# First head group of a chunked scan on TensorE: two heads in one product, unread full-height products between

## The chip, the cores and the metric

One core of a Trainium2 chip. The metric is the device time of one execution in microseconds (us), the median of three runs. The trace is one further execution, taken by the hardware profiler; all instants below are us from its start. TensorE runs at one of two clocks, 2.4 GHz (granted clock 1.00) or 1.2 GHz (0.50).

## What is computed

Two layers of token mixing (gated linear attention, HGRN2, latent attention, differential attention) and expert feed-forward. The change touches the gated scan alone:

```
S_t = diag(exp(log_g_t)) S_{t-1} + k_t^T v_t,   o_t = q_t S_t
step over chunks:  b = cumsum(g)
  scores[t,s] = sum_k q[t,k] k[s,k] exp(b[t,k] - b[s,k])   for s <= t
  out = scores @ v + (q * exp(b)) @ state
```

It runs forward and backward over 256 context tokens and then 256 latent tokens, for four GLA heads with 32 key features each and four HGRN2 heads with 64 each. Layer 0 needs all 512 tokens, layer 1 the 256 latent ones only.

## The kernel before, in words

The tokens stand in `TT` = 4 tiles of 128; `nt` is the number that a layer needs, 4 or 2. Inside a tile the scores are built by halving: a level L (64, 32, 16, 8, 4, 2, 1) covers the pairs of a query in one half and a key in the other half of a block of 2L tokens. With two directions that makes 14 (direction, level) products per head and tile; a diagonal product adds the pairs t = s. `UNITS` lists them as seven units of two levels each, and the diagonal as the eighth. Scores of keys and queries in different tiles come from the joined products (L1035, L1045).

Features lie on the partitions. Head pairs: pairs 0 and 1 hold the GLA heads at partitions 0, 32, 64 and 96 (head group c = 0, 32 rows a head), pair 2 is head group 1 and pair 3 head group 2 (64 rows a head). A float32 matmul appears in the trace as two load and matmul instructions each.

Who does what in the scan, each engine in its written order, with semaphores between:

- VectorE (`@block.vector`): arguments of the exponents of group 0 (L788 to L802); `level_keys(c, dr)` scales queries (L809) and keys (L844), then raises `ready`; `joining_keys(c)` does it for the joined products and raises `x_ready`; `gather(pr)` copies each level's scores out of PSUM into `sc` by a mask, one `copy_predicated` per head and level (L881), and the diagonal (L874), raising `unit_ev`.
- ScalarE: `exps` (L914, L917), `joining_exps` (L948, L950), `evac` (joined scores out of PSUM, raises `x_ev`), `out`.
- POOL: clears `lk`, then the exponents' arguments for groups 1 and 2, after `x_ready` 1.
- TensorE: `scores(pr)` for pair after pair. Products are written to a ring of `RB` = 6 PSUM banks, two per unit; `bank_free(n)` waits until bank n - 6 was gathered or evacuated. `output(pr)` (L1068) multiplies a pair's scores by the values; it stands behind `scores(pr + 1)`.

In the old unit (L1019 to L1026) a product of a head, level and tile has 64 query columns. The two heads lie on different rows of the array and follow each other.

Of the kernel before, what the change touches and what calls it, by code (L numbers as in the profile page):

```python
# [142 lines left out]
def build(nc, d, out):  # L143
# [17 lines left out]
    with ctx:  # L161
# [566 lines left out]
        def phase_scan(l, lo, fm, tm, hk, cum, mix):  # L728
# [7 lines left out]
            zeroed, tot_done, pool_arg, pool_key, x_ready = (  # L736
                sem(f"scan_{x}{l}") for x in ("zeroed", "tot_done", "pool_arg", "pool_key", "x_ready"))
# [6 lines left out]
            with ExitStack() as st:  # L744
# [8 lines left out]
                scx = sb(st, f"scan_scx{l}", [P, 2, 2, BANK])  # L753

# [14 lines left out]

                def key_factors(c, dr, i):  # L770
                    if c != 1:
                        return exk[:, dr, i]
                    x = NL * dr + i
                    return key_room[0][:, x] if x < 8 else key_room[1][:, x - 8]

                def key_ranges(c, dr):
                    if c != 1:
                        return [exk[:, dr]]
                    return [key_room[0][:, 7:8], key_room[1]] if dr else [key_room[0][:, 0:NL]]

                def query_arguments(eng, c, dr):
# [3 lines left out]
                    for i, L in enumerate(LEVELS):  # L785
                        mid, qa = mids(before, L), tiles(exq[:, c % 2, dr, i], L)
# [18 lines left out]
                def scale_queries(eng, c, dr):  # L805
                    q = queries(c).rearrange("p (a t) -> p a t", a=TT)
                    for i, L in enumerate(LEVELS):
                        qa = tiles(exq[:, c % 2, dr, i], L)
                        last = eng.tensor_tensor(qa, qa, halves(q[:, t0:], L, 1 - dr), ALU.mult)  # L809
                    return last  # L810

                with nc.Block() as block:
                    @block.gpsimd
                    def _(pool):
# [7 lines left out]
                        for dr in range(2):  # L822
                            key_arguments(nc.gpsimd, 2, dr).then_inc(pool_key, 1)
                        for dr in range(2):
                            pool.wait_ge(unit_mm, EN * (first[1] - 1) + 2 * UNITS_OF[dr])
                            query_arguments(nc.gpsimd, 2, dr).then_inc(pool_arg, 1)

                    @block.vector
                    def _(dve):

                        for j in range(2):
                            nc.vector.tensor_tensor(tot2[:, j], cum[:, :, 2 * j, P], cum[:, :, 2 * j + 1, P], ALU.add)\
                                .then_inc(tot_done, 1)

                        def level_keys(c, dr):
# [6 lines left out]
                            scale_queries(nc.vector, c, dr)  # L842
# [17 lines left out]

                        def gather(pr):
                            for u, unit in enumerate(UNITS):
                                for m in range(2):
                                    n = EN * pr + 2 * u + m
                                    done = 2 * NU * pr + 2 * u + m
                                    h = 2 * pr + m
                                    dst = sc[:, h % 4]
                                    dve.wait_ge(unit_mm, n + 1)
                                    if done >= 2:
                                        dve.wait_ge(unit_ev, done - 1)  # L870
                                    if u == 0 and pr >= 2:
                                        dve.wait_ge(o_mm, pr - 1)
                                    if unit is None:
                                        nc.vector.copy_predicated(dst[:, t0:], bc(maskd[:], 1, nt),  # L874
                                                                  ps[:, n % RB, lo:].rearrange("p (a t) -> p a t", a=nt)).then_inc(unit_ev, 1)
                                        continue
                                    for j, (dr, i) in enumerate(unit):
                                        L = LEVELS[i]
                                        got = ps[:, n % RB, j * 256 + t0 * HALF:(j + 1) * 256].rearrange("p (a n l) -> p a n l", a=nt, l=L)
                                        msk = bc(mask[:, NL * dr + i].rearrange("p (n l) -> p n l", l=L), 1, nt)  # L880
                                        copied = nc.vector.copy_predicated(halves(dst[:, t0:], L, 1 - dr), msk, got)  # L881
                                        if j == 0:
                                            dve_chain(dve, copied)
                                        else:
                                            copied.then_inc(unit_ev, 1)
                                c = heads[2 * pr][0]
                                if u == 3 and pr == first[c] and c:
# [11 lines left out]
                        joining_keys(0)  # L899
# [4 lines left out]
                    def _(act):  # L904
                        def exps(c):
                            for dr in range(2):
                                if c:
                                    act.wait_ge(pool_arg, 2 * (c - 1) + dr + 1)
                                else:
                                    act.wait_ge(arg_done, dr + 1)  # L910
                                if c == 2:
                                    act.wait_ge(pool_key, dr + 1)
                                e = exq[:, c % 2, dr, :, t0 * HALF:]
                                nc.scalar.activation(e, e, ACT.Exp)  # L914
                                for room in key_ranges(c, dr):
                                    e = room[:, :, t0 * HALF:]
                                    last = nc.scalar.activation(e, e, ACT.Exp)  # L917
                                last.then_inc(exp_done, 1)
# [53 lines left out]
                        exps(0)  # L972
                        for c in range(3):
                            joining_exps(c)
                            for pr in range(first[c], first[c + 1]):
                                if pr == 0:
                                    exps(1)
                                if c == 1:
                                    exps(2)
                                evac(pr)  # L980
                                if pr == 1:
                                    act.wait_ge(ready, 4)
                                if pr:
                                    out(pr - 1)
# [3 lines left out]
                    def _(pe):  # L988
# [8 lines left out]

                        def scores(pr):
# [3 lines left out]
                            for u, unit in enumerate(UNITS):  # L1002
# [3 lines left out]
                                if pr == first[c] and u in (0, 3):  # L1006
                                    dr = u // 3
                                    pe.wait_ge(ready, 2 * c + dr + 1)
                                if unit is None:
                                    if pr == first[c]:  # L1010
# [7 lines left out]
                                    continue  # L1018
                                for j, (dr, i) in enumerate(unit):  # L1019
                                    for t in range(t0, TT):  # L1020
                                        o = j * 256 + t * HALF
                                        for m, r in enumerate(rows):
                                            mm = nc.tensor.matmul(ps[:, (n + m) % RB, o:o + HALF], lk[r, dr, i, t, :],
                                                                  exq[r, c % 2, dr, i, t * HALF:(t + 1) * HALF], start=True, stop=True)
                                            if j == 1 and t == TT - 1:
                                                mm.then_inc(unit_mm, 1)  # L1026

                            n = EN * pr + 2 * NU
# [1715 lines left out]
```

## Time and profile before

| | us |
|---|---|
| median of three runs | 2969.94 (2968.53 to 2978.02) |
| the profiled execution's own time | 2969.85 |
| its span, first to last instruction | 2968.1 |
| scan of layer 0 | 206.0 to 344.8 |
| scan of layer 1 | 2038.9 to 2128.1 |
| mean granted clock over the span | 0.924 |

Over the whole span TensorE is busy 82%, VectorE 71%, ScalarE 38% and POOL 28% of the time. An engine's busy time says nothing of what ends a stretch: for that one looks at who was waited for. Matmuls overlap in the array, so the time of one is longer than the distance between two starts; costs are taken from the distance.

### The profile page before, as it was taken

How to read it: one execution, taken by the hardware profiler on the slowest of the kernel's cores; microseconds unless marked ns; L12 is line 12 of the kernel's file. 1: busy time of each engine (PE TensorE's matmuls, PEld its weight loads, DVE VectorE, ACT ScalarE, POOL GpSimd, SP SyncE). 2: the span in 40 equal slices, each digit the busy share in tenths (PEclk: the TensorE clock that was granted, in tenths of full speed). 3: DMA queues.
4: the chain of work that ended last, by engine and by line, in shares of the span. 5: the costliest groups of instructions: out<-in, count | busy, mean ns of one | idle time of the engine just before them, and what ended most of it. 6: DMA issues, size and time to landing. Idle time of an engine off the chain costs nothing. (4 is left out here: it accounts for less than half of the span.)

```text
span 2968.1 us, 36810 instructions
## 1 busy us (share of the span) xinstructions
PE 2424.4 (82%) x13114; PEld 1822.0 (61%) x13114; DVE 2110.2 (71%) x4654; ACT 1124.8 (38%) x2650; POOL 840.8 (28%) x688
## 2 busy tenths in 40 slices
PE   5979799896659888888888888688797897777776
PEld 3779565674659777777777777478556542223222
DVE  3567763499949888888888888667653898745444
ACT  3433354336633333333333333342344433334332
POOL 1004001230004434343433434103004453433431
PEclk8995799998889999999999999797798999999999
DMA  5210205264379999999999999221103999999997
GB/s 213 89 32 2 96 4 188 77 235 165 142 297 400 419 419 420 420 419 419 419 420 420 418 416 407 101 82 33 39 1 131 420 421 421 421 421 422 422 422 300
DMA packets 147671, 817.13 MB, mean 275 GB/s; under 512 B 16200, under 2 KB 17800, under 8 KB 64672
## 3 DMA queue, kind: packets, MB, share of 16 engines
q0 software_dynamic: 73728, 536.90, 43.7%
q1 hardware_dynamic: 73760, 277.87, 24.2%
q8 instruction: 105, 1.72, 0.2%
q14 instruction: 78, 0.64, 0.1%
HBM read 796.89 MB, written 17.83 MB: 274 GB/s over the span
## 5 line engine op out<-in xcount | busy, mean ns | idle before, releaser
L2412 POOL DMA_INDIRECT pair_ring<-in_uv_first,eid x256 | 395.0, 1543 | 780.9 <-DVE pair_sum L2555 274.5
L2051 PE MATMUL ps<-pair_ring,pair_diag 128*128 128x512 f32 x1024 | 475.4, 609 | 143.5 <-ACT pair_diag L2130 139.4
L2436 PE MATMUL ps<-peer_h,peer_uv 128*128 128x256 f32 x2048 | 474.8, 386 | 40.4 <-DMA peer_uv<-in_uv_dense 40.4
L2262 DVE CUSTOM_DVE_ANT_0 pair_ring<-pair_ring,hT 128x1024 f32<-128x1024 f32 x256 | 312.9, 1222 | 208.7 <-DMA pair_ring<-in_uv_rows,eid 208.6
L2051 PEld LDWEIGHTS ps<-pair_ring,pair_diag 128*128 128x128 f32 x1024 | 187.1, 192 | 421.0 <-ACT pair_diag L2130 222.6
L2436 PEld LDWEIGHTS ps<-peer_h,peer_uv 128*128 128x128 f32 x2048 | 387.3, 194 | 94.2 <-DMA peer_uv<-in_uv_dense 30.6
L119 PE MATMUL ps<-h_both 128*128 128x256 f32 x1024 | 316.0, 309 | 104.4 <-DVE h_both L2592 104.3
L2543 DVE CUSTOM_DVE_ANT_0 pair_ring<-pair_ring,hT 128x1024 f32<-128x1024 f32 x256 | 312.2, 1220 | 121.0 <-DMA pair_ring<-in_uv_first,eid 120.3
L2012 POOL DMA_INDIRECT pair_ring<-in_uv_rows,eid x256 | 270.4, 1056 | 397.9 <-PE ps L2051 360.2
L120 PE MATMUL ps<-h_both 128*128 128x256 f32 x1024 | 299.5, 292 | 0.0
L121 PE MATMUL ps<-h_both 128*128 128x256 f32 x1024 | 298.9, 292 | 0.0
L119 PEld LDWEIGHTS ps<-h_both 128*128 128x128 f32 x1024 | 205.5, 201 | 142.6 <-DVE h_both L2592 141.7
L2518 ACT ACTIVATE h_both<-peer_wt 128x256 fp32r<-128x256 f32 x128 | 53.4, 417 | 427.4 <-DVE peer_wt L2580 419.3
L120 PEld LDWEIGHTS ps<-h_both 128*128 128x128 f32 x1024 | 206.4, 202 | 0.9
L121 PEld LDWEIGHTS ps<-h_both 128*128 128x128 f32 x1024 | 206.2, 201 | 0.0
L2555 DVE SCALAR_TENSOR_TENSOR pair_sum<-pair_ring,iT,pair_sum 128x1024 f32<-128x1024 f32 x127 | 162.7, 1281 | 6.7
L2555 DVE SCALAR_TENSOR_TENSOR hT<-pair_ring,iT,hT 128x1024 f32<-128x1024 f32 x127 | 162.7, 1281 | 6.7
L2120 ACT ACTIVATE pair_dots<-pair_dots 128x2 f32<-128x2 f32 x128 | 26.0, 203 | 361.1 <-DVE pair_dots L2262 361.0
L2592 DVE TENSOR_TENSOR h_both<-peer_uv,h_both 128x1024 fp32r<-128x1024 f32 x128 | 156.4, 1222 | 3.4 <-ACT h_both L2523 1.0
L119 PE MATMUL ps<-h_hi,proj_wh 128*128 128x512 f32 (+1 forms) x304 | 116.1, 382 | 36.9 <-DVE h_lo L686 18.8
L1105 POOL TENSOR_TENSOR out_wl<-fm,out_wh 128x1024 fp32r<-128x1024 f32 x16 | 38.1, 2382 | 365.3 <-ACT out_wh L1100 365.3
L2499 ACT ACTIVATE iT<-iT 128x1 f32<-128x1 f32 x256 | 51.9, 203 | 228.6 <-DVE iT L2543 227.7
(439 smaller groups left out, 4738.5 us busy)
## 6 DMA issues: line engine op xcount, KB each, us to landing
peer_uv<-in_uv_dense SPq DMA_DIRECT2D x128, 1024.0 KB
ada_slab<-in_ada_w SPq DMA_DIRECT2D x20, 2048.0 KB, 8.2
proj_slab<-in_w_fm SPq DMA_DIRECT2D x38, 512.0 KB, 3.5
route_slab<-in_w_pq SPq DMA_DIRECT2D x32, 512.0 KB
peer_gates<-dense_stage SPq DMA_DIRECT2D x4, 4096.0 KB, 13.1
peer_gates<-peer_gates SPq DMA_DIRECT2D x16, 1024.0 KB, 21.6
fm<-in_w_out SPq DMA_DIRECT2D x16, 512.0 KB, 4.2
fm<-in_ada_w SPq DMA_DIRECT2D x3, 2048.0 KB, 11.9
```

The source lines that it names most:

```text
L119: nc.tensor.matmul(out, w[0], x[0], start=start, stop=False)
L120: nc.tensor.matmul(out, w[0], x[1], start=False, stop=False)
L121: return nc.tensor.matmul(out, w[1], x[0], start=False, stop=stop)
L2012: nc.gpsimd.indirect_dma_start(out=ring[:, s % R], out_offset=None, in_=d["uv_rows"], in_offset=bass.IndirectOffsetOnAxis(ap=eid[:, s:s + ...
L2051: mm = nc.tensor.matmul(ps[:, 4 + 2 * t + half, :], diag[:, s % DG, :], ring[:, s % R, D_MODEL + half * BANK:D_MODEL + (half + 1) * BANK], ...
L2262: nc.vector.tensor_tensor_reduce(out=row, in0=row, in1=hT[:, s // NS], scale=1.0, scalar=0.0, op0=ALU.mult, op1=ALU.add, accum_out=dots[:, ...
L2412: nc.gpsimd.indirect_dma_start(out=ring[:, s % R], out_offset=None, in_=d["uv_first"], in_offset=bass.IndirectOffsetOnAxis(ap=eid[:, s // ...
L2436: mm = nc.tensor.matmul(ps[:, e % 2, 0:n], us[:, e % SW, k, :], hw[:, k, :], start=(k == 0), stop=(k == DC - 1))
L2518: nc.scalar.activation(wh[:, e % 2], wt[:, e % 2], ACT.Copy).then_inc(whi, 1)
L2543: nc.vector.tensor_tensor_reduce(out=row, in0=row, in1=hT[:, s // NS], scale=1.0, scalar=0.0, op0=ALU.mult, op1=ALU.add, accum_out=dots[:, ...
L2555: nc.vector.scalar_tensor_tensor(out=acc[t], in0=row, scalar=dots[:, s:s + 1], in1=acc[t], op0=ALU.mult, op1=ALU.add).then_inc(sum_done, 1)
L2592: nc.vector.tensor_tensor(vl[:, e % 2], vs[:, e % SW], f32(vh[:, e % 2]), ALU.subtract).then_inc(vlo, 1)
```

## The change

1. In head group 0 a unit's product takes both heads of a pair at once: 64 rows of keys, and 128 query columns, of which the first 64 are the queries with the odd head's rows set to zero and the last 64 those with the even head's rows zero. ScalarE makes the two masked copies (`part_queries`, by the 0/1 columns of `turn`) after the queries were scaled; TensorE waits for `q_masked` ahead of units 0 and 3. A bank then holds one level of both heads; `gather_joint` reads it, alternating the heads.
2. Unread products `dense(n)` of all 128 rows and n columns into PSUM bank 7: 3 nt + 2 of 512 columns at the begin, one of 256 behind each unit of group 0, further ones of 256 around the joined products, one of 512 behind pair 0.
3. Order: `output(pr - 1)` stands ahead of the diagonal of pair pr; `joining_keys(0)` behind unit 3's gather of pair 0 (was ahead of all gathers), that of group 1 behind unit 6; `level_keys(c + 1, 0)` behind unit 6 (was unit 4); ScalarE's exponents of group 1 around `evac(0)`; the exponents' rooms of groups 1 and 2 are exchanged, and POOL computes group 2's queries and keys together.

The core of the diff:

```diff
+                def query_factors(c, dr):
+                    return exk[:, dr] if c == 1 else exq[:, 0, dr]
...
                         for dr in range(2):
-                            key_arguments(nc.gpsimd, 2, dr).then_inc(pool_key, 1)
-                        for dr in range(2):
                             pool.wait_ge(unit_mm, EN * (first[1] - 1) + 2 * UNITS_OF[dr])
-                            query_arguments(nc.gpsimd, 2, dr).then_inc(pool_arg, 1)
+                            if dr:
+                                pool.wait_ge(ready, 4)
+                            query_arguments(nc.gpsimd, 2, dr)
+                            key_arguments(nc.gpsimd, 2, dr).then_inc(pool_arg, 1)
...
+                        by_half = mask.rearrange("p (d i) t -> p d i t", d=2)[:, :, LEVELS.index(32)]
+                        nc.vector.tensor_tensor(turn[:], by_half[:, :, 0], by_half[:, :, 32], ALU.add)
...
+                        def gather_joint(pr, u):
+
+                            for j in range(2):
+                                n = 2 * u + j
+                                dve.wait_ge(unit_mm, EN * pr + n + 1)
+                                if 2 * NU * pr + n:
+                                    dve.wait_ge(even_copied, 2 * (NU - 1) * pr + n)
+                                copy_level(pr, u, j, 0).then_inc(even_copied, 1)
+                                if 2 * NU * pr + n:
+                                    dve.wait_ge(unit_ev, 2 * NU * pr + n)
+                                copy_level(pr, u, j, 1).then_inc(unit_ev, 1)
...
+                                if u == (6 if c == 1 else 3) and pr == first[c]:
                                     joining_keys(c)
-                                if u == 4 and pr + 1 == first[c + 1] and c < 2:
+                                if u == 6 and pr + 1 == first[c + 1] and c < 2:
                                     level_keys(c + 1, 0)
+                            gather_diagonal(pr)
...
                             level_keys(0, dr)
-                        joining_keys(0)
...
+                        def part_queries(dr):
+
+                            act.wait_ge(q_scaled, dr + 1)
+                            even, odd = (exq[:, m, dr, :, t0 * HALF:] for m in range(2))
+                            nc.scalar.activation(odd, even, ACT.Copy, scale=turn[:, 1:2])
+                            nc.scalar.activation(even, even, ACT.Copy, scale=turn[:, 0:1]).then_inc(q_masked, 1)
...
+                        for dr in range(2):
+                            exps(0, dr)
+                        for dr in range(2):
+                            part_queries(dr)
+                        joining_exps(0)
+                        exps(1, 0)
+                        evac(0)
+                        exps(1, 1)
+                        evac(1)
+                        act.wait_ge(ready, 4)
+                        out(0)
...
+                        def dense(n):
+
+                            nc.tensor.matmul(ps[:, 7, 0:n], ident[:], xT[:, 0, 0:n], start=True, stop=True)
...
                                     pe.wait_ge(ready, 2 * c + dr + 1)
+                                    if c == 0:
+                                        pe.wait_ge(q_masked, dr + 1)
                                 if unit is None:
+                                    if pr:
+                                        output(pr - 1)
...
+                                if c == 0:
+                                    two = slice(64 * pr, 64 * pr + 64)
+                                    for j, (dr, i) in enumerate(unit):
+                                        for t in range(t0, TT):
+                                            mm = nc.tensor.matmul(ps[:, (n + j) % RB, t * P:(t + 1) * P], lk[two, dr, i, t, :],
+                                                                  exq[two, :, dr, i, t * HALF:(t + 1) * HALF], start=True, stop=True)
+                                        mm.then_inc(unit_mm, 1)
+                                    dense(256)
+                                    continue
...
+                            if c == 0:
+                                dense(256)
                             n = EN * pr + 2 * NU
...
+                            if pr == 0:
+                                dense(256)
                             n += 2
...
+                        for _ in range(3 * nt + 2):
+                            dense(BANK)
                         for pr in range(4):
                             scores(pr)
-                            if pr:
-                                output(pr - 1)
+                            if pr == 0:
+                                dense(BANK)
                         output(3)
```

## Rows read from the trace of the kernel before

**Rows 1.** Stretches: us, busy of PE, PEld, DVE, ACT, POOL; clock, DMA; both scans.

```profile
206.00:344.80 138.80, 112.00 (x1280) 106.99 (x1280) 106.35 (x273) 44.16 (x82) 38.88 (x57) 0.67 0.01 1
2038.90:2128.10 89.20, 68.84 (x704) 63.27 (x704) 65.04 (x261) 29.69 (x70) 26.89 (x57) 0.64 0.01 1
```

**Rows 2.** The same view: most of head group 0, then the units of pair 2.

```profile
220.50:280.00 59.50, 59.42 (x540) 58.51 (x542) 43.69 (x107) 12.45 (x22) 32.81 (x56) 0.50 0.01 1
284.80:297.60 12.80, 12.80 (x228) 12.58 (x224) 10.31 (x27) 11.06 (x21) 0.00 (x0) 1.00 0.00 1
```

**Rows 3.** Groups by form, 206 to 345 us: busy us, mean ns; idle before.

```profile
L881 DVE COPY_PREDICATED scan_sc<-mask,ps 128x256 f32<-128x256 int32 x112 | 53.8, 523 | 22.5 <-PE ps L1023 20.4
L1023 PE MATMUL ps<-scan_exq,scan_lk 32*128 32x64 f32 x448 | 48.3, 416 | 15.3 <-DVE scan_lk L844 15.3
...
L1023 PE MATMUL ps<-scan_exq,scan_lk 64*128 64x64 f32 x448 | 25.4, 272 | 0.0
...
L874 DVE COPY_PREDICATED scan_sc<-maskd,ps 128x512 f32<-128x512 int32 x8 | 5.5, 746 | 0.0
```

**Rows 4.** Timeline of full-height products elsewhere: start, us; full, half, full, half clock.

```profile
1887.95 3.60 PE L502 MATMUL ps<-mix,meanD 128*128 128x512 f32 x8
...
1883.32 3.62 PE L502 MATMUL ps<-mix,meanD 128*128 128x512 f32 x4
...
829.73 2.51 PE L2426 MATMUL ps<-hot_i,hot_j 128*128 128x128 f32 x21
...
757.27 2.56 PE L2426 MATMUL ps<-hot_i,hot_j 128*128 128x128 f32 x11
```

**Rows 5.** Timeline, first product and first gather of each scan.

```profile
215.63 2.43 DVE L809 TENSOR_TENSOR scan_exq<-scan_exq,fm 128x256 f32<-128x256 f32 x7
...
217.35 1.68 ACT L917 ACTIVATE scan_exk<-scan_exk 128x1792 f32<-128x1792 f32 x1
...
220.47 24.16 PE L1023 MATMUL ps<-scan_exq,scan_lk 32*128 32x64 f32 x224 [15.29 <-DVE scan_lk L844]
...
228.58 5.44 DVE L881 COPY_PREDICATED scan_sc<-mask,ps 128x256 f32<-128x256 int32 x12
...
2045.74 0.94 ACT L917 ACTIVATE scan_exk<-scan_exk 128x896 f32<-128x896 f32 x1
...
2047.98 5.38 PE L1023 MATMUL ps<-scan_exq,scan_lk 32*128 32x64 f32 x48 [9.94 <-DVE scan_lk L844]
...
2054.42 7.09 PE L1023 MATMUL ps<-scan_exq,scan_lk 32*128 32x64 f32 x64 [1.06 <-DVE scan_sc L881]
```

**Rows 6.** Stretches again, by what TensorE did and the clock granted.

```profile
277.40:281.10 3.70, 3.69 (x16) 2.71 (x16) 3.70 (x11) 1.05 (x2) 0.69 (x2) 0.50 0.00 0
...
327.20:330.10 2.90, 0.00 (x0) 0.00 (x0) 2.83 (x8) 0.00 (x0) 0.00 (x0) 1.00 0.00 0
331.00:333.90 2.90, 2.61 (x22) 2.06 (x20) 2.80 (x7) 0.00 (x0) 0.00 (x0) 0.50 0.00 0
334.00:337.50 3.50, 3.50 (x16) 2.63 (x16) 0.95 (x2) 1.02 (x2) 0.00 (x0) 0.50 0.00 0
337.90:343.10 5.20, 5.20 (x96) 5.01 (x92) 0.00 (x0) 1.49 (x3) 0.00 (x0) 1.00 0.01 3
```

**Rows 7.** Timeline: hand-over between pairs on TensorE and VectorE, in both layers.

```profile
249.65 0.69 PE L1023 MATMUL ps<-scan_exq,scan_lk 32*128 32x64 f32 x4
...
250.92 0.64 PE L1045 MATMUL ps<-scan_xq,scan_xk 32*128 32x256 f32 x2
...
284.88 12.72 PE L1023 MATMUL ps<-scan_exq,scan_lk 64*128 64x64 f32 x224
...
286.91 8.53 DVE L881 COPY_PREDICATED scan_sc<-mask,ps 128x256 f32<-128x256 int32 x16 [3.80 <-PE ps L1023]
...
316.48 8.48 DVE L881 COPY_PREDICATED scan_sc<-mask,ps 128x256 f32<-128x256 int32 x16 [1.71 <-PE ps L1023]
...
2109.43 5.04 DVE L881 COPY_PREDICATED scan_sc<-mask,ps 128x128 f32<-128x128 int32 x16 [3.06 <-PE ps L1023]
```

More of the change, by code:

```diff
@@ L735, in phase_scan @@
                                               "x_ev", "o_mm", "o_ev"))
[L736 to L737 removed]
+            zeroed, tot_done, pool_arg, x_ready, q_scaled, q_masked, even_copied = (
+                sem(f"scan_{x}{l}") for x in ("zeroed", "tot_done", "pool_arg", "x_ready", "q_scaled", "q_masked", "even_copied"))
             heads = [(0, GLA_DK * h, GLA_DK) for h in range(4)] + [(1 + h // 2, 64 * (h % 2), 64) for h in range(4)]
@@ L785, in query_arguments @@
                     for i, L in enumerate(LEVELS):
-                        mid, qa = mids(before, L), tiles(exq[:, c % 2, dr, i], L)
+                        mid, qa = mids(before, L), tiles(query_factors(c, dr)[:, i], L)
                         if dr == 0:
@@ L859, in joining_keys @@
                             nc.vector.tensor_tensor(ksum[:, lo:], keys(c, 0)[:, lo:], keys(c, 1)[:, lo:], ALU.add).then_inc(x_ready, 1)
-                        def gather(pr):
[L862 to L887, printed above, removed]
@@ new lines, in gather_apart @@
+                        def gather_apart(pr, u):
+                            for m in range(2):
+                                dve.wait_ge(unit_mm, EN * pr + 2 * u + m + 1)
+                                dve.wait_ge(unit_ev, 2 * NU * pr + 2 * u + m - 1)
+                                if u == 0 and pr >= 2:
+                                    dve.wait_ge(o_mm, pr - 1)
+                                dve_chain(dve, copy_level(pr, u, 0, m))
+                                copy_level(pr, u, 1, m).then_inc(unit_ev, 1)
@@ new lines, in gather_diagonal @@
+                        def gather_diagonal(pr):
+                            u = NU - 1
+                            for m in range(2):
+                                n = EN * pr + 2 * u + m
+                                dve.wait_ge(unit_mm, n + 1)
+                                dve.wait_ge(unit_ev, 2 * NU * pr + 2 * u + (0 if pr < first[1] else m - 1))
+                                nc.vector.copy_predicated(sc[:, (2 * pr + m) % 4, t0:], bc(maskd[:], 1, nt),
+                                                          ps[:, n % RB, lo:].rearrange("p (a t) -> p a t", a=nt)).then_inc(unit_ev, 1)
@@ L970, in out @@
                             nc.scalar.activation(mix[:, pr, lo:], ps[:, 6 + pr % 2, lo:], ACT.Copy).then_inc(o_ev, 1)
[L972 to L982, printed above, removed]
-                                if pr:
-                                    out(pr - 1)
+                        for dr in range(2):
[9 more added lines that the diff above has]
+                        out(0)
+                        joining_exps(1)
+                        for dr in range(2):
+                            exps(2, dr)
+                        evac(2)
+                        out(1)
+                        joining_exps(2)
+                        evac(3)
+                        out(2)
                         out(3)
```

57 lines of the change are left out of this document (37 added, 20 removed).

## The prediction, made before the change was built

> **What bounds the kernel now.** I read the times of the two scans first, then the granted clock inside them, then who waits for whom. The scan of layer 0 holds 138.8 us and that of layer 1 89.2 us, with nothing of the DMA in them [rows 1]; some 2740 us lie outside and the change does not touch them. Within a scan TensorE is the engine that is hardly ever idle: 59.4 of 59.5 us between 220.5 and 280 us, and at half clock (0.50, that is 1.2 GHz) all through; the products of the next head group run at 1.00 (2.4 GHz) [rows 2]. By form: 32-row products 48.3 us for two head pairs, 64-row ones 25.4 us, for the same 448 instructions each [rows 3]. So the first head group is bound by TensorE at half clock, and the other two by VectorE, which gathers (53.8 us in all, L881) and prepares keys in the same stretches [rows 2, 3]. The prize is the clock in the first group. The whole question is whether the change keeps it.
>
> **Start of the scan.** PE issues 14 unread products of 512 columns, two instructions each. At full clock such an instruction comes every (3.60-0.59)/7 = 0.43 us, at half every (3.62-1.06)/3 = 0.853 us [rows 4]. The clock is still full when the phase begins, so 28 x 0.43 = 12.0 us, from 206.1 to 218.1. The first real product now waits for `q_masked`. ScalarE is busy with the keys' exponents until 217.35+1.68 = 219.0; then come two copies of the same 128x1792 shape, 1.7 us each and overlapping by 0.1, and VectorE's new small addition puts 0.1 us ahead of all: 222.5 us, against 220.47 before [rows 5]. In layer 1: 16 x 0.43 = 6.9 us, until 2045.8; first product 2045.74+0.94+0.85+0.95+0.1 = 2048.6, against 2047.98 [rows 5]. That is +2.0 and +0.6 us, and between the last unread product and the first real one TensorE is idle 4.4 us in layer 0 and 2.8 us in layer 1.
>
> **Does the clock live through that?** In the trace 2.9 us without any product were enough: 1.00 from 327.2 to 330.1, 0.50 from 331 [rows 6]. 4.4 us is longer; I take the clock as lost in layer 0, and in layer 1, where the gap is as long as that one, very likely too. **Does it come back?** The new product has 64 active rows. Sixty-four rows streaming without pause (two 32-row heads side by side, 3.69 of 3.70 us) left it at 0.50; all 128 rows for 2.61 of 2.90 us still left it there, and only 128 rows at 3.50 of 3.50 brought it back [rows 6]. At half clock a new unit is four fifths 64-row products and one fifth a 128-row one: weaker than the second stretch. So the group stays at half until `output(0)`, 3 to 5 us of dense work.
>
> **A unit, at half clock.** Old: 16 products in layer 0, 32 instructions, 24.16/7 = 3.41 us (24.16 is the time of pair 0's 224 instructions) [rows 5]. New: 8 products of 128 columns, 16 instructions. A 128x128 instruction comes every (2.56-0.42)/10 = 0.214 us at half and every (2.51-0.28)/20 = 0.112 at full clock [rows 4]: 3.42 us. So halving the instructions gains nothing: before, the two heads ran side by side. The unread 256 columns add 2 x 0.427 = 0.85: 4.27 us, +0.86 each. At full clock it would be 1.79+0.43 = 2.22. Layer 1 has half the tiles: 1.71+0.85 = 2.56 against 1.71.
>
> The Trainium skill (TensorE: Matmul & The Clock Gate, "Part 3: Packing small matmuls") says that a weight load overlaps running products only when its row group differs; all joint products of a pair use the same rows. By that each of 16 instructions would also show its load of 128 columns, 0.107 us at half clock, and a unit would cost 1.7 us more. Rows 4 disagree: there the rows are the same each time, and the pitch is that of the columns alone.
>
> **Layer 0, sum.** Start +2.0. Fourteen units x 0.86 = +12.0. Other unread products: behind pair 0 256+256+512 columns at half, 0.85+0.85+1.71 = 3.4; behind pair 1 0.6 (0.43 to 0.85): +4.0. Before, pair 1 (rows 64 to 127) began at 249.65 while pair 0's last products (rows 0 to 63) ran until 251.56 [rows 7]; the unread product with all rows closes that: +1.9. `output(0)` now stands before pair 1's diagonal instead of behind pair 1; it is the same work, but it brings the clock back, so pair 1's last products cost half (L1045, 16 instructions of 256 columns, 3.5 [rows 6] to 1.75; the 32 of 128 columns before them, as many columns in all, the same; `output` itself some 0.5 less): -4.0. Pair 2 starts at 284.88+15.9 = 300.8 [rows 7].
>
> From there VectorE sets the pace. It gathered 2.0 us behind TensorE [rows 7]. Now `level_keys(1,0)` waits until after unit 6: with two rounds of seven per call, 2.43 a round of which 0.08 overlaps the next [rows 5], and a diagonal of 5.5/4 = 1.4 [rows 3], 4.7+1.4+4.7 = 10.8 us behind the last unit's gather at 293.9, that is 304.7 where 300.8+2.0 was the old distance: +1.9. Its idle 1.7 us before pair 3 goes (TensorE is ahead there): -1.7 [rows 7]. `output(2)` leaves the end, where two outputs took 5.20 us [rows 6], for a stretch in which TensorE waits for VectorE: -2.6. What it hides in: the gathers of pair 3; if that cover were gone, +2.6 again. `joining_keys(0)` (3.6 us: four such rounds from 215.63 end at 225.0, and the gather began at 228.58 [rows 5]) moves behind the fourth gather, and POOL's arguments, ScalarE's `exps(1,0)` and behind that `evac(0)` slide with it; at half clock TensorE is not that fast: x_ready comes at some 244, the exponents by 256, when the joined products are just done. Cost zero; with full clock 2 to 4 us. POOL's c=2 keys wait for `ready` 4: hidden by pair 2's 29 us. Last, TensorE is waiting more in pairs 2 and 3 and may lose the clock once more often; between 0 and +3.4 (two units at half), I take +1.5. Sum: 15.9+1.9-1.7-2.6+1.5 = **+15.0 us**.
>
> **Layer 1.** Start +0.6; fourteen units x 0.85 = 12.0, less a wait of 1.1 us for gathers in pair 0 that goes with the moved joining keys [rows 5, 7]: +10.8; unread products +4.0; lost overlap, taken as in layer 0, +1.9; pair 1's end at full clock -3.4; VectorE's start 0.7 nearer; its idle 3.1 us before pair 3 goes [rows 7]; `output(2)` -1.8 (a third fewer products than layer 0's). Sum **+8.3 us**. Together +23.3 on the profiled execution of 2969.85 us (its span is 2968.1), which is 0.1 from the median 2969.94: **2993 us**.
>
> Ends of what the trace does not show: the two masked copies (a Copy with a column as scale) 1.7 us each, at worst twice, +3.4 per layer, hidden behind nothing; an interleaved gather (128-column blocks read in halves, waits one instruction further apart) between -0.1 and +0.1 us per copy, off the path at half clock. The predicate, bank count and evacuations are the same.
>
> **Rivals.**
> 1. *The clock holds* (faster). Place: the gap ahead of unit 0. If ScalarE were done sooner or the unread products later, so that the gap is well below the 2.9 us that lost it, the group runs at 2.22 us a unit: 14 x -1.19 = -16.7, start +2.0, other unread +2.0, overlap +1.9, tails at full -7, new waits for `joining_keys` and `evac(0)` +4: -13.8 at pair 2; VectorE then gives back 1.5 net, `output(2)` -2.6: -15. Layer 1 the same way: units -5.5, old wait -1.1, start, unread and overlap +4.5, tails and output -7, VectorE's waits +3, idle and `output(2)` -4.9: -11. **2944 us.** For it: 64-row products held 1.00 for 12.8 us [rows 2]. Against: the sum of the gap. Chance 17%.
> 2. *The clock comes back between the pairs* on the 512 columns behind pair 0, so pair 1 runs at full: 7 x 2.05 = 14.3 less 3 for waits in layer 0, 8.7 less 1.2 in layer 1: +4.5, **2974**; in one layer only 2982 to 2986. Against: the 2.61 of 2.90 us. For: L1045, then 1.7 us of all rows, without a pause. Chance 17%.
> 3. *The load is not hidden* (the rule of Part 3): 14 x 1.7 + 14 x 0.85 = +36 more, **3029**. A mechanism that rows 4 deny. Chance 3%.
> 4. My forecast, clock lost and half all through group 0: chance 63%, own range 2982 to 3001 (VectorE-bound tail 0 or +3.4 in both layers, copies, when exactly the clock rises).
>
> This kernel's measurement can tell about 0.3% (9 us) from no change. Rival 1 is faster, with a little of rival 2 in one layer and a lucky layer 1: 0.18. Same (2961 to 2979): most of rival 2, 0.15. Slower 0.67. The range reaches to rival 1's upper half and a little over the forecast: 2946 to 3001.
>
> **What would show it.** Clock 0.50 when the first new L1023 starts near 222.5, about 4.4 us after the last unread product; pair 0's units 4.2 to 4.3 us apart and a matmul pitch of 0.213; clock back only in `output(0)` near 296; pair 2 starting near 301; VectorE not idle before pair 3; the scan of layer 0 near 154 us and that of layer 1 near 97. Wrong, if the clock stays 1.00 at unit 0 in layer 0 (then unit pitch 2.2 and a scan near 124), or if it rises during the units.

## The result, and the profile after

The changed kernel takes 3013.86 us in the median of 4 runs (3006.01 to 3023.63), the kernel before 2969.34 (2968.53 to 2978.02, 4 runs): a ratio of 1.0146, 95% interval 1.0131 to 1.0161. It is slower, as forecast, but by 44 us instead of 23, and above the range (2946 to 3001). The profiled execution took 3011.62 us, its span is 3009.8.

First the same windows as in [rows 1]: both scans, then the stretch of head group 0 in each at half clock.

```profile
206.40:369.70 163.30, 148.92 (x1120) 121.78 (x1120) 104.86 (x274) 50.88 (x86) 38.88 (x57) 0.70 0.00 1
2063.10:2172.10 109.00, 98.14 (x644) 73.53 (x644) 64.25 (x262) 33.17 (x74) 26.52 (x57) 0.69 0.00 1
222.30:300.00 77.70, 76.97 (x296) 61.19 (x297) 31.46 (x77) 16.89 (x28) 24.57 (x42) 0.50 0.00 1
2072.30:2126.00 53.70, 52.98 (x176) 37.20 (x176) 20.39 (x79) 10.99 (x24) 15.34 (x42) 0.50 0.00 0
```

The scans take 163.3 and 109.0 us where they took 138.8 and 89.8: +24.5 and +19.2, together 43.7. (Here and below a scan lasts until the next stage's first instruction; the 89.2 of [rows 1] end 0.6 us earlier, with the scan's own last one.) The stretch between them is 1693.4 us (1694.1 before), the one behind them 837.7 (839.4). So the whole loss lies inside the scans. In both, head group 0 runs at 0.50 with TensorE 99% busy, as it did before.

The timeline of TensorE at the start of each scan shows why. Columns: start, duration, engine, line, operation, tiles, shape, count, and in brackets the idle time before and what ended it.

```profile
206.47 12.26 PE L1045 MATMUL ps<-xT,ident 128*128 128x512 f32 x28 [0.90 <-PEq L473]
223.03 3.75 PE L1076 MATMUL ps<-scan_exq,scan_lk 64*128 64x128 f32 x16 [4.31 <-ACT scan_exq L957]
226.71 1.22 PE L1045 MATMUL ps<-xT,ident 128*128 128x256 f32 x2
227.86 3.78 PE L1076 MATMUL ps<-scan_exq,scan_lk 64*128 64x128 f32 x16
231.57 1.22 PE L1045 MATMUL ps<-xT,ident 128*128 128x256 f32 x2
...
2063.19 7.10 PE L1045 MATMUL ps<-xT,ident 128*128 128x512 f32 x16 [0.90 <-PEq L473]
2073.02 2.05 PE L1076 MATMUL ps<-scan_exq,scan_lk 64*128 64x128 f32 x8 [2.73 <-ACT scan_exq L957]
2075.00 1.22 PE L1045 MATMUL ps<-xT,ident 128*128 128x256 f32 x2
2076.15 2.07 PE L1076 MATMUL ps<-scan_exq,scan_lk 64*128 64x128 f32 x8
```

The unread products end, TensorE waits 4.31 and 2.73 us for the masked queries, and the granted clock is 0.50 from 222.3 and from 2072.3. Up to here all is as forecast. But a unit takes 231.57-226.71 = 4.86 us, not 4.27, and in layer 1 3.15 (2.07 and 1.22 overlap), not 2.56. Both are 0.59 too long. Look at the starts: from the first joint product of a unit to its unread one it is 231.57-227.86 = 3.71 us for 16 instructions, 0.29 more than 16 x 0.2135; from there to the next unit 227.86-226.71 = 1.15, 0.30 more than 2 x 0.427 [rows 4]. Each instruction keeps its pitch except at the two places where the row shape changes from 64 to 128 rows or back.

The clock comes back only in `output(0)`, in layer 0 at 307.6 (rows of the changed kernel):

```profile
301.93 1.22 PE L1045 MATMUL ps<-xT,ident 128*128 128x256 f32 x2
303.08 0.70 PE L1134 MATMUL ps<-scan_sc,tm 128*64 128x128 f32 x4
...
305.27 1.50 PE L1134 MATMUL ps<-scan_scx,tm 128*64 128x128 f32 x12
...
306.97 1.16 PE L1134 MATMUL ps<-scan_scx,tm 128*64 128x128 f32 x12
...
312.60 12.95 PE L1085 MATMUL ps<-scan_exk,scan_lk 64*128 64x64 f32 x224
```

Twelve of its instructions take 1.50 us at 305.27 and 1.16 at 306.97, across the rise; the 64-column units of pair 2 behind it run at 1.00, as before the change [rows 2].

### The profile page after: what moved, and what is told of

It is laid out like the page before. It is cut to its first block and busy times, and to the rows that moved or that the text cites. A ratio compares the mean times of both kernels' runs of the same rounds, so it can differ in the third digit from the quotient of the medians.

```text
span 3009.8 us, 36384 instructions
## 1 busy us (share of the span) xinstructions
PE 2495.0 (83%) x12894; PEld 1850.8 (61%) x12894; DVE 2108.4 (70%) x4656; ACT 1134.7 (38%) x2658; POOL 838.0 (28%) x688
## 5 line engine op out<-in xcount | busy, mean ns | idle before, releaser
L119 PEld LDWEIGHTS ps<-h_both 128*128 128x128 f32 x1024 | 203.6, 199 | 142.6 <-DVE h_both L2660 141.5
L120 PEld LDWEIGHTS ps<-h_both 128*128 128x128 f32 x1024 | 204.2, 199 | 0.7
L121 PEld LDWEIGHTS ps<-h_both 128*128 128x128 f32 x1024 | 203.8, 199 | 0.0
L881 DVE COPY_PREDICATED scan_sc<-mask,ps 128x256 f32<-128x256 int32 (+1 forms) x224 | 83.4, 434 | 80.2 <-PE ps L1076 77.5
```

Of the source, the lines that this page charges most:

```text
L119: nc.tensor.matmul(out, w[0], x[0], start=start, stop=False)
L120: nc.tensor.matmul(out, w[0], x[1], start=False, stop=False)
L121: return nc.tensor.matmul(out, w[1], x[0], start=False, stop=stop)
L881: return nc.vector.copy_predicated(halves(sc[:, h % 4, t0:], L, 1 - dr), msk, got)
```

## The experiments

Eleven kernels; each ratio is against the kernel before on the same chip (e1 to e4 share one, e5 to e9 one, e10 and e11 one). "Scan 0" and "scan 1" are read from each trace as above. Outside the scans, where nothing was changed, the profiled executions differ by up to 12 us (the stretch between the scans took 1693 to 1694 us in the kernel before, in after, e4, e5, e9 and e10, 1698 in e7, 1701 to 1702 in e1, e8, e11 and e12, 1705 in e2 and e3; the one behind them 838 to 846), so mechanisms are judged by the scans. Each scan time is that of one execution.

```
kernel              median us (range)            before   ratio [95%]              scan 0  scan 1
before                                                                             138.8    89.8
after               3013.86 (3006.01-3023.63)    2969.34  1.0146 [1.0131, 1.0161]  163.3   109.0
e1 no unit dense    2983.29 (2979.39-2992.54)    2979.28  1.0018 [1.0007, 1.0029]  144.8    87.9
e2 dense, 64 rows   3007.53 (2998.26-3010.06)    2979.28  1.0086 [1.0064, 1.0107]  158.4    98.8
e3 dense split      3045.32 (3038.34-3052.63)    2979.28  1.0213 [1.0196, 1.0230]  171.9   125.5
e4 bridge           2961.66 (2956.69-2968.54)    2979.28  0.9941 [0.9919, 0.9962]  132.1    84.0
e5 order alone      2967.45 (2962.34-2974.85)    2972.19  0.9983 [0.9972, 0.9993]  141.9    84.0
e7 bridge, no dense 2968.46 (2955.74-2972.62)    2972.19  0.9982 [0.9970, 0.9993]  134.9    85.4
e8 bridge all       2959.55 (2953.84-2963.72)    2972.19  0.9955 [0.9941, 0.9968]  127.2    84.1
e9 old, bridged     2970.85 (2969.40-2976.13)    2972.19  0.9999 [0.9989, 1.0008]  139.0    93.0
e10 every second    2962.42 (2952.79-2964.99)    2971.37  0.9965 [0.9951, 0.9979]  135.0    78.2
e11 every third     2958.53 (2951.26-2960.37)    2971.37  0.9950 [0.9937, 0.9963]  135.0    77.8
e12 evac bridged    2949.14 (2941.48-2955.12)    2973.85  0.9915 [0.9898, 0.9933]  127.9    78.2
```

**The missing 0.59 us a unit: e1, e2, e3.** Three edits of the unread product behind the unit.

```diff
 # e1
-                                    dense(256)
 # e2: ident[two, :], xT[two, 0, 0:256] instead of all 128 rows
-                                    dense(256)
+                                    dense(256, two)
 # e3
                                         mm.then_inc(unit_mm, 1)
-                                    dense(256)
+                                        dense(128)        # inside the loop over j: after each level
```

e1: 

> The changed kernel without the unread 256-column product behind each unit of group 0 (14 per layer); all else as changed. Theory A (a switch between products of 64 and of 128 active rows stalls the array, about 0.59 us per unit at half clock, on top of the 0.85 us of streaming): a unit falls from 4.86 to 3.42 us in layer 0 and from 3.15 to 1.71 in layer 1, 14 x 1.44 per layer, so some 40 us less than the changed kernel, near 2973. Theory B (the missing 0.59 us belongs to a unit's begin or to the joint products and has nothing to do with the switch): only 0.85 per unit goes, 24 us less, near 2990. Both: the clock stays at half through group 0.

e2: 

> The changed kernel with the unread 256-column product behind a unit on the unit's own 64 rows instead of all 128 rows: same columns, no change of rows. Theory A: the 0.59 us per unit goes, the 0.85 stays: unit 4.27 us in layer 0, 2.56 in layer 1, 2 x 14 x 0.59 = 16.5 us less than the changed kernel, near 2997. Theory B (a 256-column product costs 1.15 us whatever its rows): unit stays at 4.86, near 3014. Clock at half in both.

e3: 

> The changed kernel with two unread products of 128 columns per unit, one behind each level, instead of one of 256: same columns, twice the switches. Theory A: 0.59 us more per unit (4.86 to 5.45 in layer 0, 3.15 to 3.74 in layer 1), 16.5 us more than the changed kernel, near 3030. Theory B: no change, near 3014.

The timelines of e1, e2 and e3, one fence each:

```profile
221.29 24.23 PE L1076 MATMUL ps<-scan_exq,scan_lk 64*128 64x128 f32 x112 [4.36 <-ACT scan_exq L957]
```

```profile
226.13 1.06 PE L1045 MATMUL ps<-xT,ident 64*128 64x256 f32 x2
226.98 3.62 PE L1076 MATMUL ps<-scan_exq,scan_lk 64*128 64x128 f32 x16
230.39 1.06 PE L1045 MATMUL ps<-xT,ident 64*128 64x256 f32 x2
```

```profile
224.97 2.07 PE L1076 MATMUL ps<-scan_exq,scan_lk 64*128 64x128 f32 x8
226.97 0.79 PE L1045 MATMUL ps<-xT,ident 128*128 128x128 f32 x2
```

All three start behind a gap of the same size and run at 0.50. Without the unread product a unit costs 3.42 us. With one of the same 256 columns on the unit's own 64 rows it costs 230.39-226.13 = 4.26, the forecast sum of columns, and nothing more: 0.85 from the unread product to the next unit, where the changed kernel shows 1.15. With the same columns split in two, so that there are twice as many changes of shape, it costs 2 x 2.72 = 5.45, that is 1.18 over the columns, twice 0.59. So the stall belongs to the change of shape and not to the product, how many columns it streams, or its data.

By the ratios to the kernel before, e1 takes 38 us less than the changed kernel, e2 18 less and e3 20 more, where 40, 16.5 and 16.5 were worked out. Two scans are far from the sum, and in both the clock differs too. In e2's layer 0 (4.9 us less instead of 8.3) the clock is at 0.50 from 337.8 on, through most of pair 3. In e3's layer 1 (16.5 us more instead of 8.3) it comes back only at 2180.5, behind pair 2, whose 112 instructions take 12.21 us where the changed kernel's take 7.4.

Two rows say more of the stall. In the changed kernel the last unread product of pair 1 (301.93, `128*128` in the view: 128 rows, 128 columns of the array) is followed by `output(0)` (303.08, `128*64`: 128 rows, 64 columns). The rows are the same, and yet the distance is 1.15 us as in front of 64-row products. So a change of the array's columns stalls TensorE too at that end, and the rows are only what the experiments varied. And the kernel before had a change of shape at half clock where one could have looked:

```profile
277.41 3.78 PE L1045 MATMUL ps<-scan_xq,scan_xk 32*128 32x256 f32 x16
281.12 0.69 PE L1068 MATMUL ps<-scan_sc,tm 128*64 128x128 f32 x4
```

Sixteen instructions of 256 columns, two side by side, should take 8 x 0.427 = 3.42 us; it is 3.71 to the next shape, 0.29 more. (TensorE had paused for 0.3 us ahead of 277.41, so how much of the 0.29 is the change's this row does not say.)

**The gap: e4.** The unread products at the begin run on until the queries are there.

```diff
-                        for _ in range(3 * nt + 2):
+                        for _ in range(19 if nt == 4 else 12):
                             dense(BANK)
```

> The changed kernel with 19 (layer 0) and 12 (layer 1) unread 512-column products at the begin instead of 14 and 8, so that they end with q_masked and TensorE is not idle ahead of unit 0. Theory C (the idle 4.3 and 2.7 us lost the clock, and the 64-row units with the unread products hold it): group 0 at 1.00, unit near 2.5 us in layer 0, scan of layer 0 near 130 us instead of 163 and that of layer 1 near 85 instead of 109, in all 45 to 57 us less than the changed kernel, 2957 to 2969. Rival: the clock goes in the waits behind pair 0 (ScalarE's exponents of group 1 ahead of evac(0)) and pair 1 runs at half: 20 to 25 us less, near 2990. Rival: the clock does not depend on the gap, no change or 1 us more.

Windows of e4 in layer 0 and 1, then its timeline at the first unit:

```profile
220.00:285.60 65.60, 64.38 (x623) 53.33 (x622) 53.26 (x134) 28.77 (x52) 32.81 (x56) 1.00 0.01 1
2036.00:2084.00 48.00, 47.43 (x368) 34.11 (x367) 36.45 (x152) 21.97 (x49) 21.82 (x57) 1.00 0.00 1
```

```profile
221.51 2.02 PE L1076 MATMUL ps<-scan_exq,scan_lk 64*128 64x128 f32 x16
223.46 0.70 PE L1045 MATMUL ps<-xT,ident 128*128 128x256 f32 x2
```

The granted clock stays at 1.00 through all of head group 0, and the result turns from 1.5% slower to 0.6% faster with nothing else changed. The gap is what cost the clock. A unit is 2.61 us and not the 2.22 of rival 1: the change of shape is paid at the full clock too, 0.39 us there and back (2.61 less 16 x 0.112 + 0.43). What remains is lost later: TensorE waits 2.31 us for pair 2's joining keys and 2.20 for pair 3's first bank, and pair 3 runs at half clock:

```profile
293.03 1.16 PE L1067 MATMUL ps<-fm,mix 64*128 64x128 f32 x16 [2.31 <-DVE mix L868]
...
299.01 23.85 PE L1085 MATMUL ps<-scan_exq,scan_lk 64*128 64x64 f32 x224 [2.20 <-DVE scan_sc L912]
```

**What the order alone is worth: e5.** After's order and homes of the factors, with group 0's products and gathers as before, no masked queries and no unread products.

```diff
-                                if c == 0:
-                                    two = slice(64 * pr, 64 * pr + 64)
-                                    ...
-                                    dense(256)
-                                    continue
...
-                                    if c == 0:
-                                        pe.wait_ge(q_masked, dr + 1)
...
-                                if c == 0:
-                                    gather_joint(pr, u)
-                                else:
-                                    gather_apart(pr, u)
+                                gather_apart(pr, u)
```

> The new order, the new homes of the factors and output(pr - 1) ahead of the diagonal product, but the first head group as in the kernel before: one product per head on 32 rows, one gather copy per head and unit as before, no masked queries, no unread products. It prices all that the change moves beside its products. Forecast (the prediction's own terms: -4.0 us at pair 1's tail, +1.9 VectorE, -1.7 idle, small in layer 1): scans 3 to 5 us shorter than the kernel before in layer 0, 0 to 2 us in layer 1, time 4 to 6 us under it. Rival (the order itself is what lengthens the scans): slower than the kernel before, scans longer, which would take the blame from the row shapes.

Layer 1 is 5.8 us shorter, layer 0 3.0 longer. Together the scans are 2.8 us shorter and the time 4.7, so the rival does not hold; but both forecasts by layer are misses (3 to 5 and 0 to 2 us shorter). Up to pair 2 the order does bring something: it starts 77.2 us into the scan (78.9 before). But then pair 3 takes 23.84 us at half clock where the kernel before took 12.72 (e5's timeline):

```profile
302.36 1.16 PE L1055 MATMUL ps<-fm,mix 64*128 64x128 f32 x16 [2.31 <-DVE mix L866]
...
308.35 23.84 PE L1064 MATMUL ps<-scan_exq,scan_lk 64*128 64x64 f32 x224 [2.20 <-DVE scan_sc L907]
```

Ahead of it stand the two waits that e4 has too, and the half clock costs TensorE 11.1 us. Not all of that is the scan's: in e8 below, where the same waits are filled, 10.7 us less in pair 3 make layer 0 only 4.9 shorter. By that, layer 0 of e5 would be some 137 us, 2 shorter than before. This is an estimate; no run of e5 with the waits filled was made. The changed kernel escaped it: its clock was at 0.50 from 331.5 to 338.4 instead, and pair 3 started at 338.82 and ran at 1.00 until 352.0.

**Which products hold the clock: e7, e9.** e7 is e4 without `dense(256)` behind the units; e9 is the kernel before with unread products only at the begin.

```diff
 # e9
+                        for _ in range(18 if nt == 4 else 11):
+                            nc.tensor.matmul(ps[:, 7, 0:BANK], ident[:], xT[:, 0, 0:BANK], start=True, stop=True)
                         for pr in range(4):
                             scores(pr)
```

e7: 

> e4_bridge without the unread product behind each unit; the unread products at the begin still run until the first real one is ready, so the units start at the full clock. Theory A (the switch between 64-row and 128-row products stalls TensorE, the rest is products at their own pitch): if the 64-row products alone hold the clock, a unit takes 1.71 us, 0.9 less than in e4, so layer 0's scan is up to 12 us under e4's 132, as far as VectorE's copies keep up. Theory C2 (the 64-row products alone don't hold it, the dense one behind each unit is what does): the granted clock falls to 0.50 some microseconds into pair 0 and units take 3.42 us from there, time between 2965 and 2985, near e1.

e9: 

> The kernel before with unread 512-column products alone, 18 in layer 0 and 11 in layer 1, up to its first real product; its units stay one product per head on 32 rows. It asks whether a clock kept over the gap is enough by itself. Theory (products on 32 rows do not hold the clock): 1.00 at the first unit, 0.50 some microseconds on, a gain of a few microseconds at most, 2962 to 2970. Rival (the gap was all that cost the clock): pairs 0 and 1 run at 1.00 with units of 1.71 us, as far as VectorE's copies keep up, and the time is under 2955, which would make the two-head products needless.

Windows of e7 (pair 0, then the rest of group 0), and of e9 (the first units, the rest):

```profile
221.20:237.50 16.30, 14.74 (x134) 14.12 (x136) 16.30 (x48) 7.59 (x18) 3.40 (x6) 1.00 0.00 1
237.70:272.00 34.30, 34.30 (x164) 30.51 (x164) 15.84 (x35) 8.61 (x9) 20.99 (x36) 0.50 0.01 1
```

```profile
222.30:225.80 3.50, 3.50 (x65) 3.50 (x64) 3.50 (x12) 1.50 (x7) 0.00 (x0) 1.00 0.02 5
226.00:283.90 57.90, 56.24 (x506) 54.55 (x506) 41.97 (x100) 10.88 (x13) 32.79 (x56) 0.50 0.01 1
```

In e9 the 32-row units inherit 1.00 and lose it 3.6 us on, and the time is that of the kernel before: a bridge alone gives nothing, the rival falls. (Part of the little gain goes in the bridge itself: the first unit of layer 0 starts 15.7 us into the scan instead of 14.4.) In e7 the 64-row units keep 1.00 for the whole of pair 0; it falls at 237.6, when TensorE has waited 1.56 us for VectorE and goes on with products on 32 rows, and pair 1 runs at half (24.26 us instead of 12.74 for the same 112 instructions). Both of its theories are partly right. What in the new unit holds the clock is not separated: an old one is 32 instructions of 64 columns on 32 rows, side by side in pairs, a new one 16 of 128 columns on 64. That pair 2's products, 64 columns on 64 rows, kept 1.00 for 12.8 us [rows 2] speaks for the rows.

**The other waits: e8, e10, e11, e12.** e8 is e4 with unread products on bank 6 at the two waits of pairs 2 and 3; e10 and e11 then thin out those behind the units; e12 is e10 with one more bridge.

```diff
 # e8: pair 2 ahead of the diagonal, pair 3 ahead of its first unit
+                        def bridge(k):
+                            pe.wait_ge(o_ev, 1)
+                            for _ in range(k):
+                                nc.tensor.matmul(ps[:, 6, 0:256], ident[:], xT[:, 0, 0:256], start=True, stop=True)
...
+                            if pr == 3:
+                                bridge(2 * nt - 3)
...
+                                    if pr == 2:
+                                        bridge(2 * nt - 3)
 # e10 (e11: u in (2, 5))
+                                    if u in (1, 3, 5):
                                         dense(256)
 # e12: e10 and
+                                    if nt == 4 and pr == 1 and u == 0:
+                                        for _ in range(6):
+                                            dense(256)
```

e8: 

> e4_bridge with five unread 256-column products in layer 0 (one in layer 1) at each of the two places where TensorE waits in the last two pairs: ahead of pair 2's diagonal products and ahead of pair 3's first unit. Theory (a gap loses the clock there too): the clock, back at 1.00 in output(1), is kept over the gap of 2.3 us and the next of 2.2 us, and pair 3's 14 units start at 1.71 us instead of 3.41; 5 to 9 us off layer 0's scan unless VectorE's copies end last, 0 to 2 in layer 1, time 2952 to 2958. Rival (the 64-column products lose the clock by themselves): granted clock back at 0.50 within pair 3, and at most 3 us gained over e4.

e10: 

> e8_bridge_all with the unread product behind units 2, 4 and 6 of a pair alone instead of behind all seven, four less in each pair of the first head group. Theory A prices each one (its two records of 0.21 us and two changes of row shape) at some 0.8 us at the full clock, from units of 2.61 us in e4 against 1.82 us in e7: if the clock holds, pairs 0 and 1 are 2 x 4 x 0.8 = 6.4 us shorter less what VectorE's copies then hold back (about 2.04 us for a unit), so layer 0's scan near 122 to 124 us and the time 4 us under e8. If three in seven don't hold the clock it falls inside pair 0 or 1, units take 3.4 us from there and the scan is 5 to 12 us longer than e8's.

e11: 

> As e10 with only two of seven, behind units 3 and 6. Full clock held: 1 to 2 us less than e10 at most, since VectorE's copies set the pace of a unit near 2.04 us. Not held (nearer to e7, where none of seven lost the clock at the end of pair 0): the granted clock at 0.50 in pair 1 and a scan of 128 to 135 us in layer 0.

e12: 

> e10_every_second with six more unread 256-column products in layer 0 behind the first unit of pair 1, where TensorE waited 2.64 us for ScalarE's evacuation of the joined products and the clock went to 0.50 at the end of that wait. Theory (the gap lost the clock there, not the thinner unread products): pair 1 runs at 1.00 with two units and one unread product in 4.4 us, output(0) starts at some 263 us instead of 273.5, the scan of layer 0 takes 124 to 128 us, VectorE setting the pace behind it, and the time is 2949 to 2955. Rival (three unread products in seven units are too few): the clock falls within pair 1 all the same, and the scan stays at 132 to 136 us.

e8's timeline at pair 3:

```profile
298.18 2.42 PE L1050 MATMUL ps<-xT,ident 128*128 128x256 f32 x10
300.53 10.94 PE L1094 MATMUL ps<-scan_exq,scan_lk 64*128 64x64 f32 x192
311.68 2.00 PE L1094 MATMUL ps<-scan_exq,scan_lk 64*128 64x64 f32 x32 [0.21 <-DVE scan_sc L881]
```

Pair 3's units fall from 23.85 to 13.1 us; of these 10.7 the scan shows 4.9, since VectorE's gathers set the end (busy 29.5 of 30.0 us from 290 to 320). The time does not show it: 2959.55 us is 1.6 above the expected range, and the ratio, 0.9955, is not under e4's 0.9941. Only the scan of layer 0 says that e8 is better there. In e10 pair 0 is as cheap as worked out, and then pair 1 loses the clock, in a wait for ScalarE's evacuation; e12 fills it. e10's rows, then e12's:

```profile
243.98 2.05 PE L1085 MATMUL ps<-scan_exq,scan_lk 64*128 64x128 f32 x16
248.67 3.52 PE L1085 MATMUL ps<-scan_exq,scan_lk 64*128 64x128 f32 x16 [2.64 <-ACT scan_scx L1005]
252.12 1.22 PE L1045 MATMUL ps<-xT,ident 128*128 128x256 f32 x2
```

```profile
245.88 2.86 PE L1045 MATMUL ps<-xT,ident 128*128 128x256 f32 x12
248.67 2.05 PE L1085 MATMUL ps<-scan_exq,scan_lk 64*128 64x128 f32 x16
250.65 0.70 PE L1045 MATMUL ps<-xT,ident 128*128 128x256 f32 x2
```

The second unit starts at 248.67 in both; with the wait filled it takes 2.05 us, without 3.52, and so does all of pair 1 (clock at 1.00 until 275.9). So it was the wait that lost pair 1, not the thinner unread products; e11's fall at the same place (249.1) reads the same way, though only e10's was undone. Layer 1, where no such wait stands, gained in e10 and e11 at once (84.1 to 78.2 and 77.8). e12 beats the kernel before by 0.85% (0.67 to 1.02%) and the changed one by about 2.3% (1.0146/0.9915, on two chips). e10's sum for layer 0 failed only in part by that wait: it came to 135.0 where 122 to 124 was worked out, and e12, without the wait, to 127.9. That is no better than e8 with all its unread products (127.2): e12's pair 2 loses the clock at 275.9 and gets it back at 293.0. So in layer 0 the thinning has gained nothing, and e12's lead over e8 in the scans is that of layer 1 (78.2 for 84.1).

## Why the prediction was too low

The forecast's mechanism is what happened: clock lost in the gap, half all through group 0, clock back in `output(0)`, loss confined to the scans. Its steps for layer 0 and 1, from the two profiled executions:

```
                                      forecast        measured
start of the first real product       +2.0  +0.6      +2.2  +0.8
fourteen units (layer 1: less wait)  +12.0 +10.8     +20.1 +18.8
behind pair 0 (unread, overlap)       +5.3  +5.3      +6.8  +6.7
behind pair 1 (output(0), unread)     -3.4  -2.8      -1.8  -3.7
pair 2 to the end                     -0.9  -5.6      -2.8  -3.4
sum                                  +15.0  +8.3     +24.5 +19.2
```

**The step that failed** is "The unread 256 columns add 2 x 0.427 = 0.85: 4.27 us". The term is 1.44 us: 0.85 for the columns and 0.59 for two changes of row shape. Over 14 units 0.59 makes 8.3 us per layer; the table's rows miss 8.1 and 8.0, together 16 of the 20 us. The same stall stands behind pair 0, where three unread products follow products on 32 rows: 3 x 0.59 = 1.8 against the 1.5 missed there in layer 0. I had taken the pitch from rows in which all products have one shape [rows 4], and no bound for a mixed stream was set, though the kernel before had a place to look (281.12 above); the prediction bounded the copies and the gather, but not this.

**Part 3's rule.** Of the weight load the Trainium skill (TensorE: Matmul & The Clock Gate, "Part 3: Packing small matmuls") says that it overlaps only when the row group differs, or, in the paragraph on its mechanism, when it goes to the background weight buffer. Measured, the joint products of one row group keep a pitch of 24.23/112 = 0.216 us at half clock, so the load stays hidden, as rows 4 said; which of the two cases this is, no row tells. The cost stands at the opposite place, where the row shape changes.

**Points that held.** The gap 4.31 us for 4.4, and 2.73 for 2.8. Pitch of a joint product 0.213: halving the instructions gained nothing (e1's units, 3.42 us, are the old ones, 3.42 to 3.45). The cost of losing the clock is settled by e4. Small ones that did not: behind pair 1 in layer 0, `output(0)` itself ran 4.5 us at half clock before the rise, so less of the tail was at full than I gave it (+1.6). VectorE's side in layer 0 came out 1.9 better than forecast, in layer 1 2.2 worse; that these cancel is luck. The old unit was written as 24.16/7 = 3.41 us; the quotient is 3.45, and by the starts a unit is (244.41 - 220.47)/7 = 3.42, so the slip moves the sum by 0.1 us a layer. Rival 2 did not come: the 512 unread columns behind pair 0 left the clock at 0.50. **Rival 1** priced the held clock at 2944 us; e4, which is that case, shortens the scans by 6.7 and 5.8 us against 15 and 11 forecast. Of the 13.5 us between, 14 x 0.39 per layer is the stall again (10.9), and pair 3 at half clock in layer 0 was not in the sum (4.9 by e8); the two make 2.3 us too much, and what stands against that was not traced.

## What to carry to other kernels

Unread products only pay if nothing interrupts them: make them last until the first real operand is ready, and then look for the next wait of TensorE, since it can give the whole gain back. Price a product in a mixed stream by rows in which its neighbours have other rows, and use as few changes of row shape as hold the clock. Judge such a change by the stretch it touches: the 12.5 us that e4 took from the scans stand beside nearly as much scatter elsewhere (11.6 us between the scans, from one kernel to another).

## What the runs showed of the hardware that was not expected

- A change between 64-row (or 32-row) and 128-row products, all of 128 columns of the array, stalls TensorE by 0.29 to 0.30 us at 1.2 GHz each way (0.59 there and back, in units of both layers, and twice that in e3), and by 0.39 there and back at 2.4 GHz (e4). Between products on the same 64 rows, of different columns and data, it is nothing (e2). An unread product of 128 rows takes its 1.15 us also in front of `128*64` products, which use 128 rows too (after, 301.93 to 303.08).
- Units with products on 32 rows alone lost a full clock 3.6 us after they began (e9), although TensorE was busy 3.50 of 3.50 us; joint products on 64 rows kept it through their 12.7 us (e7); it fell at 237.6, after a wait of 1.56 us and products on 32 rows.
- The full clock was lost in waits of 2.73 us (after, layer 1) and 2.64 us (e10), and kept over waits of 0.30 (e8), 1.58 (e10) and 2.31 us (e4, e5). In e4 and e5 it fell behind a second wait, of 2.20 us, that began 3.8 us after the one of 2.31 had ended. Among the 64-column products of pair 2 it fell right behind waits of 0.70 to 0.73 us in e4, e8 and e12, but not behind one of 0.68 in e10; what made the difference stays open.
- Stretches that no edit touched took 1693 to 1705 us from one profiled execution to another.
